# Experts of a hybrid encoder layer: the low part of five two-row-tile weight chunks moves from VectorE to GpSimd

## What is computed

```python
def expert(args):
    w1e, w3e, w2e, ie, ge = args
    xe = jnp.take(xt, ie, axis=0)                 # 32 prompt + 64 sample rows per expert
    hid = jax.nn.silu(xe @ w1e) * (xe @ w3e)
    return (hid @ w2e).astype(jnp.float32) * ge[:, None]
out = jnp.zeros((n, D), jnp.float32).at[idx.reshape(-1)].add(ye.reshape(-1, D))
```

## Time and profile before

| | |
|---|---|
| median of 3 runs | 2114.09 us (2113.16 to 2114.78) |
| the profiled execution | 2114.79 us, its span 2113.0 us |
| TensorE busy | 2021.7 us, 96% |
| VectorE busy | 1609.9 us, 76% |
| ScalarE busy | 1337.5 us, 63% |
| GpSimd busy | 76.4 us, 4% |
| HBM read and written | 597 MB and 20 MB |

### The profile page before, as it was taken

How to read it: one execution, slowest core, us unless ns; L and a number is a source line. 1 busy time by engine, 2 the same in 40 slices (tenths; PEclk the granted TensorE clock), 3 DMA queues, 4 the chain that set the end, 5 groups by cost and what they waited for, 6 DMA issues and landing times.

```text
span 2113.0 us, 27664 instructions
## 1 busy us (share of the span) xinstructions
PE 2021.7 (96%) x10732; PEld 1548.7 (73%) x10732; DVE 1609.9 (76%) x1135; ACT 1337.5 (63%) x1017; POOL 76.4 (4%) x38
## 2 busy tenths in 40 slices
PE   6999997969679999999999999999999999999998
PEld 5899996758557777777777777777767777777775
DVE  4247764673468888888888888888888888888886
ACT  4234432661357777777777777777777777777774
POOL 0000000000200000000000000000000000000000
PEclk9999998979889999999999999999999999999999
DMA  5222223035469999999999999999999999999994
GB/s 154 73 68 78 89 75 141 3 126 196 161 226 380 373 372 389 364 389 360 387 368 383 375 364 395 358 397 365 386 372 375 386 360 396 357 390 367 383 381 147
DMA packets 190066, 618.27 MB, mean 293 GB/s; under 512 B 12224, under 2 KB 35776, under 8 KB 190016
## 3 DMA queue, kind: packets, MB, share of 16 engines
q1 hardware_dynamic: 186432, 604.99, 76.3%
q0 software_dynamic: 3584, 12.58, 2.6%
HBM read 597.09 MB, written 20.45 MB: 292 GB/s over the span
## 4 chain that ended last, share of the span: by engine, by line
PE 93%; DVE 3%; DMA 2%; ACT 1%; issue 0%; SPq 0%; POOL 0%; ACTq 0%; POOLq 0%; DVEq 0%
PE pair L517 28%; PE pair L519 28%; PE pair L518 28%; PE pair L578 2%; PE pair L811 1%; DMA q_t<-queries_and_keys 1%; PE pair L651 1%; PE pair L740 1%; PE pair L673 1%; PE pair L763 1%; PE pair L636 0%; DMA hg<-projected 0%; DMA x_in<-x 0%; PE pair L618 0%; PE pair L662 0%
## 5 line engine op out<-in xcount | busy, mean ns | idle before, releaser
L1506 DVE TENSOR_TENSOR chunk_low<-ring,chunk_high 128x2048 fp32r<-128x2048 f32 (+1 forms) x382 | 1175.5, 3087 | 225.1 <-ACT chunk_high L1050 225.1
L1050 ACT ACTIVATE chunk_high<-ring 128x3072 fp32r<-128x3072 f32 (+1 forms) x384 | 979.4, 2559 | 213.7 <-PE pair L519 213.4
L517 PE MATMUL pair<-chunk_high,xe_high 128*96 128x512 f32 (+1 forms) x1536 | 579.5, 377 | 1.3 <-DVE xe_low L1500 1.3
L519 PE MATMUL pair<-chunk_high,xe_low 128*96 128x512 f32 (+1 forms) x1536 | 575.3, 375 | 0.0
L518 PE MATMUL pair<-chunk_low,xe_high 128*96 128x512 f32 (+1 forms) x1536 | 573.1, 373 | 0.0
L517 PEld LDWEIGHTS pair<-chunk_high,xe_high 128*96 128x96 f32 x1536 | 248.2, 162 | 90.0 <-DVE chunk_low L1506 2.5
L519 PEld LDWEIGHTS pair<-chunk_high,xe_low 128*96 128x96 f32 x1536 | 247.7, 161 | 90.3
L518 PEld LDWEIGHTS pair<-chunk_low,xe_high 128*96 128x96 f32 x1536 | 248.6, 162 | 87.4
L517 PE MATMUL pair<-chunk_high,hid_high 128*96 128x512 f32 x704 | 280.2, 398 | 0.0
L519 PE MATMUL pair<-chunk_high,hid_low 128*96 128x512 f32 x704 | 277.1, 394 | 0.0
L518 PE MATMUL pair<-chunk_low,hid_high 128*96 128x512 f32 x704 | 275.8, 392 | 0.0
(11 more groups left out here) (202 smaller groups left out, 1828.7 us busy)
## 6 DMA issues: line engine op xcount, KB each, us to landing
ring<-w SPq DMA_DIRECT2D x288, 1536.0 KB, 9.3
ring<-w SPq DMA_DIRECT2D x96, 1024.0 KB, 8.3
raw_w<-w_in SPq DMA_DIRECT2D x16, 1024.0 KB, 5.6
projected<-stage SPq DMA_DIRECT2D x36, 128.0 KB, 1.7
wo_raw<-w_out SPq DMA_DIRECT2D x8, 512.0 KB, 3.2
x_in<-x SPq DMA_DIRECT2D x6, 512.0 KB, 8.2
queries_and_keys<-qk_raw SPq DMA_DIRECT2D x8, 384.0 KB, 2.7
x_again<-x SPq DMA_DIRECT2D x6, 512.0 KB, 5.0
```

What stands on the lines that cost most here:

```text
L517: pe.matmul(dst, a_high, b_high, start=first, stop=False)
L519: return pe.matmul(dst, a_low, b_high, start=False, stop=last)
L1050: act.activation(ch[c % SPLIT][:, 0:n], ring[c % RING][:, 0:n], ACT.Copy).then_inc(ch_done, 1)
L1506: dve.tensor_tensor(cl[c % SPLIT][:, 0:n], ring[c % RING][:, 0:n], ch[c % SPLIT][:, 0:n].bitcast(F32), ALU.subtract).then_inc(cl_done, 1)
```

## The change

GpSimd gets the low parts of chunks 5, 8, 11, 17 and 21 of every expert, each 128 by 2048, counted by a semaphore of its own, `pool_low`. Chunk 2, the sixth of that size, stays on VectorE. TensorE and SyncE wait for `pool_low` at these five chunks and for `cl_done`, whose count now runs over the other 19, at the rest. On GpSimd the scatter of an expert is issued at the start of the next one, behind the gather, and the wait for its landing stands behind chunk 5. The buffers, the loads, the matmuls and ScalarE's program are as they were.

```diff
--- before.py
+++ after.py
@@ -94,6 +94,9 @@
 HID_AT = {LAST[b, 1] + 2 + g: (b, g) for b in range(NB) for g in range(2)}
 XE_AT = {len(UP) + 3: 0, len(UP) + 4: 1}
 T_PER_EXPERT = 2 * NB + 2
+LOW_BY_POOL = [5, 8, 11, 17, 21]
+POOL_LOWS = len(LOW_BY_POOL)
+DVE_LOWS = CHUNKS - POOL_LOWS
 
 
 def build(nc, x, norm1, w_in, lbf, lbb, hgw, qw, kw, lams, subw, w_out, norm2, rw, w1, w3, w2,
@@ -335,6 +338,7 @@
     cl_done = sem("chunk_low_done")
     early_low = sem("early_chunk_low_done")
     used = sem("chunks_used")
+    pool_low = sem("chunk_low_by_pool")
     silu_done = sem("silu_done")
     hid_done = sem("hid_done")
     t_mm = sem("t_mm")
@@ -387,6 +391,13 @@
 
     def chunk_size(c):
         return UP[c][3] * BLOCK_W[UP[c][0]] if c < len(UP) else W2_KT[c - len(UP)] * D
+
+    def wait_low(eng, e, c):
+
+        if c in LOW_BY_POOL:
+            eng.wait_ge(pool_low, e * POOL_LOWS + (LOW_BY_POOL.index(c) + 1))
+        else:
+            eng.wait_ge(cl_done, e * DVE_LOWS + (c + 1 - sum(1 for p in LOW_BY_POOL if p < c)))
 
     def load_piece(sp, hc):
 
@@ -503,10 +514,10 @@
                 load_chunk(sp, 0, c + RING)
             with sp.Fori(0, EXPERTS - 1) as e:
                 for c in range(EARLY, CHUNKS + EARLY):
-                    sp.wait_ge(cl_done, e * CHUNKS + (c + 1))
+                    wait_low(sp, e + c // CHUNKS, c % CHUNKS)
                     load_chunk(sp, e, (c + RING) % CHUNKS, (c + RING) // CHUNKS)
             for c in range(EARLY, CHUNKS - RING):
-                sp.wait_ge(cl_done, (EXPERTS - 1) * CHUNKS + c + 1)
+                wait_low(sp, EXPERTS - 1, c)
                 load_chunk(sp, EXPERTS - 1, c + RING)
 
 
@@ -770,7 +781,7 @@
 
         def expert(e, last):
             for c in range(CHUNKS):
-                pe.wait_ge(cl_done, e * CHUNKS + (c + 1))
+                wait_low(pe, e, c)
                 hi, lo = chunk_view(ch[c % SPLIT], c), chunk_view(cl[c % SPLIT], c)
                 if c < len(UP):
                     b, m, k0, n = UP[c]
@@ -1508,7 +1519,7 @@
 
         def expert(e, last):
             for cc in range(2, CHUNKS + 2):
-                if cc < CHUNKS or not last:
+                if (cc < CHUNKS or not last) and cc % CHUNKS not in LOW_BY_POOL:
                     chunk_low(e, cc)
                 c = cc - 2
                 if c < len(UP) and c == LAST[UP[c][0], 1]:
@@ -1552,16 +1563,33 @@
         pool.sem_inc(y_free, 1)
         pool.wait_ge(xt_out, 16 * TILES)
         gather(0)
+        def scatter(e):
+            pool.wait_ge(y_ev, e + 2)
+            if e >= 1:
+                pool.wait_ge(y_out, 16 * e)
+            pool.indirect_dma_start(out=out, out_offset=bass.IndirectOffsetOnAxis(ap=token[:, e:e + 1], axis=0),
+                                    in_=y_sb[:, :], in_offset=None, bounds_check=T - 1,
+                                    compute_op=ALU.add).then_inc(y_out, 16)
+
+        def chunk_low(e, c):
+            n = chunk_size(c)
+            pool.wait_ge(ch_done, e * CHUNKS + c + 1)
+            pool.tensor_tensor(cl[c % SPLIT][:, 0:n], ring[c % RING][:, 0:n], ch[c % SPLIT][:, 0:n].bitcast(F32),
+                               ALU.subtract).then_inc(pool_low, 1)
+
         for e in range(EXPERTS):
             if e + 1 < EXPERTS:
                 pool.wait_ge(t_mm, e * T_PER_EXPERT + 2)
                 gather(e + 1)
-            pool.wait_ge(y_ev, e + 2)
-            pool.indirect_dma_start(out=out, out_offset=bass.IndirectOffsetOnAxis(ap=token[:, e:e + 1], axis=0),
-                                    in_=y_sb[:, :], in_offset=None, bounds_check=T - 1,
-                                    compute_op=ALU.add).then_inc(y_out, 16)
-            pool.wait_ge(y_out, 16 * (e + 1))
-            pool.sem_inc(y_free, 1)
+            if e >= 1:
+                scatter(e - 1)
+            for c in LOW_BY_POOL:
+                chunk_low(e, c)
+                if e >= 1 and c == LOW_BY_POOL[0]:
+                    pool.wait_ge(y_out, 16 * e)
+                    pool.sem_inc(y_free, 1)
+        scatter(EXPERTS - 1)
+        pool.wait_ge(y_out, 16 * EXPERTS)
 
     moe.close()
     perm.close()
```

## The result

The changed kernel takes 2144.31 us (median of 4 runs, 2142.76 to 2145.71) against 2114.44 us for the kernel before, in the same session: a ratio of 1.0142, with an interval of 1.0130 to 1.0154. That is 29.9 us slower; the forecast was 2145, within 2120 to 2170. The profiled execution has a span of 2141.7 us.

The account below looks back on a forecast made before the run. TensorE's matmul stream was taken as the bound; losses of 0.7, 0.62 and 0.53 us at chunks 5, 6 and 12, 1.85 an expert, 30 us over 16, with half a us for a handover, gave 2145, range 2120 to 2170.

Parts of the forecast that it names:

- The bound: Experts' stage: TensorE's matmul stream sets the time; taking 11.5 of VectorE's 80.14 us an expert gains nothing.
- Chunk 5: GpSimd's low part takes 4.43 us against VectorE's 2.29 and ends too late for TensorE: 0.7 us lost in each expert.
- Chunk 6: VectorE's low part waits until GpSimd's for the chunk before has ended, and is late for TensorE: 0.62 us an expert.
- Chunk 12: VectorE's low part waits until GpSimd's for chunk 11 has ended, and is late for TensorE: 0.53 us an expert.
- The sum: The losses at chunks 5, 6 and 12 add to 1.85 us an expert, 30 us over 16 experts.
- half a us for a handover: Allowance in the forecast time for handovers between GpSimd and VectorE, each of which may add a tenth or so.
- Low(8): GpSimd's low part of chunk 8 ends at 1003.8, wanted by TensorE at 1005.71, so it has room.
- Exclusion: VectorE's and GpSimd's low parts: an operation waits until the other engine's has ended; between 2135 and 2160, chance 0.55.
- side-by-side rival: GpSimd and VectorE do not disturb each other; only chunk 5 is late, 11 us, 2125; chance 0.25.
- the one in which GpSimd yields: VectorE's low parts go first and stretch GpSimd's; 64 us for chunk 5 alone, 2179 or more; chance 0.11.
- The moves: GpSimd's gather and scatter DMAs in their new places, with the landing wait behind chunk 5: cost nothing.
- the ring: SyncE's loads into the ring buffers: chunk 11's load starts 2.2 us later but lands with 5 us left; cost nothing.

Follow-up runs that it names:

- the run with chunks 8, 17 and 21: Changed kernel with only the low parts of chunks 8, 17 and 21 on GpSimd, 5 and 11 back on VectorE: 2115.22 us, 1.0007 of the kernel before.
- short fills: Changed kernel with GpSimd writing zeros (2048, 512 and 512 elements) in place of the five chunks' subtractions: 2115.09 us beside 2115.79 for the kernel before.
- copies: Changed kernel with GpSimd copying the ring buffer (one operand read) in place of the five chunks' subtractions: 2115.30 us, 0.9997 of the kernel before.
- the fills: Changed kernel with GpSimd writing zeros (2048, 2048 and 768 elements) in place of the five chunks' subtractions: 2124.20 us, 1.0049 of the kernel before.
- the moves alone: Changed kernel with all low parts on VectorE, only the gather and scatter DMAs and the landing wait moved: 2114.16 us, 0.9999 of the kernel before.

## Why the prediction was right

**The bound.** TensorE's stream sets the time, and VectorE's freed time is worth nothing: the run with chunks 8, 17 and 21 frees 6.9 us an expert and gains none, and the runs with short fills and with copies free 11.5 and gain none.

**Chunk 5**, forecast 0.7, measured 0.87. The mechanism is as given, in 15 experts of 16: the forecast had it come back in each, and in the last, with no table load ahead of the silu, it does not. The term was small by 0.17 because two thirds of 6.65 us left out a fixed part: 4.63 was measured, and the two sizes together give (6.65 - 4.63)/1024 = 2.0 ns an element and some 0.6 us fixed. The figure of the Trainium skill (GPSIMD Engine Reference, section Performance versus the Vector engine), 4497 ns for an addition, is nearer than mine and still 0.13 short of the trace.

**Chunk 6**, forecast 0.62, measured 0.52. The forecast moved chunk 6's due time by 0.70, though the low(5) that it used made chunk 5 late by 0.73, so its own terms give 0.59. A blocked instruction loses 0.13 us less than it is held (1.76 of 1.89), and the weight load follows 0.11 behind low(6) where it followed 0.05 behind low(5): 0.59 - 0.13 + 0.06 is 0.52. The length of low(5) drops out, as it moves low(6) and the due time alike. **Chunk 12**, forecast 0.53, measured 0.47: low(12) is held for 0.96 and grows by 0.84.

**The sum** came closer than its terms: 0.17 too little at chunk 5 was met by 0.10 and 0.06 too much at chunks 6 and 12, so 1.85 was forecast for an expert and 1.86 measured. That is luck. So is part of the agreement of 2145 with 2144.31, since sixteen full stalls and half a us for a handover were counted where the profile shows fifteen, and one of 0.9.

**Low(8)** was missed. The prediction had GpSimd undisturbed there and took a GpSimd low part over 5 us for a sign of yielding. It reads 5.89 because VectorE's low(7) had begun first, which is exclusion too; it cost no time, as low(8) still ended at 1013.57 and chunk 8's first weight load came at 1014.56.

**Exclusion**, the choice that the trace of before could not make and that had 0.55, is shown three ways: durations that grow by about the overlap on both engines, their return to 3356 ns when GpSimd only writes, and copies that are held too. By the Trainium skill's rule (SBUF — State Buffer, section Who interferes with whom) a VectorE instruction with two SBUF inputs contends with GpSimd instructions that read SBUF and not with ones that only write it; the traces agree on both counts, low(6) reading 5.12 us beside the subtraction and 3.36 beside the fills. The side-by-side rival fell with it, at 2125, and so did the one in which GpSimd yields: GpSimd's low(5) kept its 4.63 us with VectorE waiting behind it. Whichever begins first keeps its length.

**The moves and the ring** were counted at nothing, and the moves alone cost nothing. That the ring's later loads cost nothing was not tested by itself; but no wait of ScalarE for a load appears in the changed kernel's experts, and the three terms leave nothing over.

No version faster than the kernel before came out of the study, and with TensorE busy for 94.00 of 94.00 us, and its waits for low parts 5.1 us in all, little was to be had by moving them.

## What to carry to other kernels

Work taken from an engine that isn't the bound bought nothing here; ask whether the slower engine meets each due time, one by one, since one chunk of five made 72% of this loss. VectorE's two-operand SBUF reads and GpSimd's SBUF reads ran one after the other in every trace here, so where two of them meet, moving work to GpSimd puts its longer time ahead of VectorE's next operation. If work has to go to GpSimd, place it where the due time is far and the next VectorE read isn't near, as chunks 17 and 21 were. And look at the first and the last turn of a loop by themselves: here the last lacked the table load that made chunk 5 late.

## What the runs showed of the hardware

A blocked instruction of either engine starts in the trace when its own semaphore wait ends (low(6) at 1000.69, 0.02 us behind the end of its high part) and carries the hold in its length: 5.12 for 3.36 us on VectorE, 5.89 for 4.63 and 3.19 for 1.91 on GpSimd. A handover costs nothing; the blocked one even makes up 0.12 to 0.14 us (1.76 of 1.89, 0.84 of 0.96, 1.26 of 1.39). The hold goes by reads: fills of 4.50 us on GpSimd left VectorE's two-operand reads at 3356 ns, and VectorE's product with one operand in PSUM took 1.21 us beside low(8).
